# Modulation rows 4 to 9 of a hybrid diffusion step: summed on VectorE and GpSimd instead of by 32-column products on TensorE

## The chip, the cores and the metric

One core of a Trainium2 chip runs the whole step. The metric is device time in microseconds (us); the median of three runs of the kernel before is 1153.03 us. Engines: TensorE (PE, its weight loads PEld), VectorE (DVE), ScalarE (ACT), GpSimd (POOL), SyncE (SP, whose queue issues most transfers).

## The reference, cut to what matters

```python
mod = silu(c) @ w_mod + b_mod            # latent tokens; silu(c_ctx) for context tokens
shift1, scale1, gate1, shift2, scale2, gate2 = split(mod, 6)
h = rms_norm(x, g_attn) * (1 + scale1) + shift1
x = x + gate1 * token_mixing(h)          # attention, two branches, output projection
h = rms_norm(x, g_ffn) * (1 + scale2) + shift2
x = x + gate2 * expert_choice_ffn(h)     # 16 experts
y = rms_norm(x, g_final)
```

`w_mod` is 1024 x 6144 in float32. The kernel works on it in twelve "rows" of 512 columns: rows 0 to 3 are shift1 and scale1, rows 4 and 5 gate1, rows 6 and 7 shift2, rows 8 and 9 scale2, rows 10 and 11 gate2. Each row is wanted for two vectors: v = 0, the latent condition, and v = 1, the context condition. There are 512 latent and 128 context tokens, in five tiles of 128.

## The kernel before

The program of each engine is written out by hand, with semaphores between the engines; each engine executes its own list in order.

The dense part is a list of 15 matrix products, `GEMMS`, numbered j = 0 to 14. Numbers 5 to 14 follow attention: ga0, wa0, gb0, wb0 (5 to 8) make columns 0 to 511 of the merged branches, ga1, wa1, gb1, wb1 (9 to 12) columns 512 to 1023, out0 and out1 (13, 14) are the output projection. The g products have eight blocks of 128 rows of weights, the w products four. Weights arrive in chunks of 1 MB (`STREAM`, one after the other through a ring of four buffers `raw`, issued by SP as the buffer's last user finishes). A chunk is two halves `hh`; each half is passed once over the five token tiles t, with two blocks and three float32r matmuls of 512 columns for each (high times high, high times low, low times high). ScalarE makes the high part of a half (`split_hi`), VectorE the low part (`split_lo`, 1024 columns), both two halves ahead of TensorE (`half_ahead`). A product's result lies in one of six PSUM banks. For a w product VectorE frees the bank (`branch_of`: a multiply, and for gb's partner wb also an add that makes `merged`), for a g product ScalarE does (`gate_of`). So a place in the order is a triple (j, hh, t).

Rows 4 to 9 of the modulation are twelve more chunks of that stream (`MODS_AFTER`: after which chunk which of them follows). `mod_chunk` (line 787) runs each as four matmuls with the two condition vectors as stationary operand, two columns of each of four 32-column groups of the array. After a row's second chunk VectorE copies the 128 x 512 partial result out of bank 7 (`keep_row`, line 1910, counted in `s_row`).

`TURNS` says before which place TensorE does a small extra task through PSUM bank 6, one after the other: "merged" transposes one tile of the merged branches, "turn" n brings row n into columns (line 857), "spread" n, v spreads a gate1 row over all partitions (line 861). VectorE finishes each at the same place of its own list: `merged_lo` the low part of the transposed tile, `add_bias` for a turn (`turned_row`), and for a spread an add onto `gate1`, which holds the bias and is loaded by GpSimd after product 11 (lines 2325 to 2327, awaited through `s_gb`). `residual_of` multiplies the output projection by `gate1`.

`gate_step` (line 1945) sums rows 10 and 11 on VectorE already: for each block of 128 rows a scalar-times-tensor-plus-tensor instruction over 512 columns.

In the stretch between attention and the end of product 11 GpSimd has nothing to do: its list stands at the wait of line 2325. The experts follow the dense part: `expert_block` on TensorE, with weights through twenty 1 MB buffers.

Of the kernel before, what the change touches and what calls it, by code (L numbers as in the profile page):

```python
# [100 lines left out]
def halves_of(j):  # L101
# [13 lines left out]
TURNS = {(9, 1, 0): ("merged", 0), (9, 1, 2): ("merged", 1), (9, 1, 4): ("merged", 2), (9, 2, 1): ("merged", 3),  # L115
         (9, 2, 3): ("merged", 4), (10, 0, 2): ("turn", 6), (11, 0, 2): ("turn", 7), (12, 0, 2): ("turn", 8),
         (12, 0, 4): ("spread", 4, 0), (12, 1, 1): ("spread", 4, 1), (12, 1, 3): ("spread", 5, 0),
         (13, 0, 0): ("spread", 5, 1), (13, 0, 2): ("turn", 9), (13, 0, 3): ("merged", 5), (13, 0, 4): ("merged", 6),
# [4 lines left out]
GATE_STEPS = {_p: (_s // 4, _s % 4) for _s, _p in enumerate(GATE_AT)}  # L123
MOD_TURNS = [e for e in TURN_LIST if e[0] != "merged"]
# [113 lines left out]
def build(nc, x_prompt, x_sample, cache_attn_k, cache_attn_v, cache_diff_k, cache_diff_v, c, c_ctx,  # L238
# [5 lines left out]
    with ctx:  # L244
# [170 lines left out]
        s_actfn = sem("s_actfn"); s_vecfn = sem("s_vecfn"); s_vecturn = sem("s_vecturn"); s_modq = sem("s_modq"); s_tab = sem("s_tab"); s_tab2 = sem("s_tab2"); s_vec = sem("s_vec"); s_x = [sem(f"s_tokens{t}") for t in range(NT)]  # L415
# [6 lines left out]
        s_row = sem("s_row"); s_post = sem("s_post"); s_mod = sem("s_mod"); s_scale = sem("s_scale")  # L422
# [7 lines left out]
        s_kc = [sem("s_kc0"), sem("s_kc1")]; s_vc = sem("s_vc"); s_vac = sem("s_vac")  # L430
# [2024 lines left out]
```

## Time and profile before

| | us |
|---|---|
| three runs | 1152.22, 1153.03, 1153.11 |
| span of the profiled execution, first to last instruction | 1148.9 |
| what lies around the span, by the median of the runs | 4.1 |
| TensorE busy in the span | 1099.2 (96%) |
| VectorE busy | 543.8 (47%) |
| ScalarE busy | 369.2 (32%) |
| GpSimd busy | 154.4 (13%) |

The profile is one execution, taken by the hardware. The profiled execution's own device time is not listed beside its span; the runs stand 4.1 us above the span. All times below are us from the span's start, durations us unless marked ns. Matmuls overlap in the engine, so for TensorE the distance between starts tells more than a duration. In the span, attention ends near 328, products 6 to 12 run from 360.6 to 523, the experts from 625 on.

### The profile page before, as it was taken

The page shows a single profiled execution, that of the slowest core. Times are in us where ns is not written, and L with a number is a line of the kernel's source. Part 1 is how long each engine was busy: PE and PEld are TensorE (multiplying, and loading weights), DVE is VectorE, ACT ScalarE, POOL GpSimd, SP SyncE. Part 2 cuts the span into 40 slices and gives each one's busy share as a digit, 9 for nine tenths or more (in the row PEclk, how much of TensorE's full clock was granted, in tenths as well). Part 3 has the DMA queues.
Part 4 walks back from the last instruction along what each step waited for, and adds up shares of the span by engine and source line. Part 5 has one row for each costly group of instructions (what it writes and reads, how often), then busy time and mean ns, then how long its engine had stood idle before and what let it go on. Part 6 is the DMA issues. An engine that isn't in the chain of part 4 may idle for free.

```text
span 1148.9 us, 28297 instructions
## 1 busy us (share of the span) xinstructions
PE 1099.2 (96%) x12561; PEld 835.7 (73%) x12561; DVE 543.8 (47%) x993; ACT 369.2 (32%) x856; POOL 154.4 (13%) x213
## 2 busy tenths in 40 slices
PE   6999998999999999999998999999999999999983
PEld 4679887777877777777878777777777777777662
DVE  3575458889968232325877133332233222333235
ACT  4343236777754123122162321222222222211103
POOL 1342440000000000002012111111111111110020
PEclk9999999999999999999999999999999999999996
DMA  9952232212052543368989999999999999999993
GB/s 359 306 224 73 74 74 58 44 25 47 1 198 73 184 146 102 119 220 285 322 301 365 371 403 406 406 406 411 413 407 406 408 406 408 405 408 408 407 322 135
DMA packets 87467, 302.53 MB, mean 263 GB/s; under 512 B 27329, under 2 KB 28610, under 8 KB 62258
## 3 DMA queue, kind: packets, MB, share of 16 engines
q1 hardware_dynamic: 79680, 273.38, 62.0%
q0 software_dynamic: 6528, 20.10, 6.1%
q10 hardware_dynamic: 1138, 7.25, 1.7%
q8 instruction: 99, 1.62, 0.6%
q14 instruction: 22, 0.18, 0.0%
HBM read 276.86 MB, written 18.60 MB: 257 GB/s over the span
## 4 chain that ended last, share of the span: by engine, by line
PE 80%; DVE 6%; DMA 6%; issue 3%; ACT 3%; ACTq 0%; SPq 0%; POOLq 0%; POOL 0%; DVEq 0%
PE ps L1194 39%; PE ps L775 9%; PE ps L777 9%; PE ps L776 9%; PE ps L1001 3%; PE ps L985 2%; DVE neg_max L1794 2%; DMA x_dram<-y_row,rows_t 2%; PE ps L1024 1%; PE ps L1020 1%; DMA x_dram<-xn_p 1%; DVE q_lo_t L1786 1%; PE ps L797 1%; DMA raw<-in_w_in_dram 1%; DMA x_f<-x_dram 1%
## 5 line engine op out<-in xcount | busy, mean ns | idle before, releaser
L2122 DVE SCALAR_TENSOR_TENSOR y_row<-ps,gates,gate_q 32x256 f32<-32x256 f32 (+1 forms) x184 | 88.3, 480 | 237.4 <-PE ps L1194 234.9
L1549 ACT ACTIVATE h_t<-ps 128x256 f32<-128x256 f32 x48 | 15.0, 384 | 371.7 <-PE ps L1194 371.7
L775 PE MATMUL ps<-w_hi,ht 128*128 128x512 f32 (+1 forms) x320 | 124.8, 390 | 0.0
L777 PE MATMUL ps<-w_hi,ht 128*128 128x512 f32 (+1 forms) x320 | 121.8, 381 | 0.0
L776 PE MATMUL ps<-raw_lo,ht 128*128 128x512 f32 (+1 forms) x320 | 121.7, 380 | 0.0
L1194 PE MATMUL ps<-late,xe 128*32 128x256 f32 x1824 | 100.3, 379 | 0.0
L542 DVE TENSOR_TENSOR raw_lo<-raw,w_hi 128x1024 fp32r<-128x1024 f32 x48 | 57.7, 1225 | 78.5 <-ACT w_hi L537 78.0
L1194 PEld LDWEIGHTS ps<-late,xe 128*32 128x32 f32 x1824 | 71.9, 110 | 26.5
L2379 POOL DMA_INDIRECT xg<-x_dram,rows x48 | 46.1, 960 | 318.7 <-PE ps L1194 290.5
L537 ACT ACTIVATE w_hi<-raw 128x1024 fp32r<-128x1024 f32 x48 | 48.8, 1052 | 122.3 <-DMA raw<-in_w_in_dram 67.5
L1539 ACT ACTIVATE xe<-xt,mods_q 128x64 f32<-128x64 f32 x240 | 78.0, 423 | 7.6 <-DVE gates L2106 7.6
L1194 PE MATMUL ps<-raw,xe 128*32 128x256 f32 x1392 | 80.0, 379 | 0.0
L775 PEld LDWEIGHTS ps<-w_hi,ht 128*128 128x128 f32 x320 | 60.1, 188 | 16.6 <-issue 5.2
L1194 PE MATMUL ps<-raw_gate,xe 128*32 128x256 f32 x1248 | 71.3, 379 | 0.0
L1194 PEld LDWEIGHTS ps<-raw,xe 128*32 128x32 f32 x1392 | 54.9, 110 | 20.2
L777 PEld LDWEIGHTS ps<-w_hi,ht 128*128 128x128 f32 x320 | 60.0, 188 | 12.8
L1194 PE MATMUL ps<-late,ht 128*32 128x256 f32 x1200 | 67.5, 379 | 1.1 <-issue 1.1
L776 PEld LDWEIGHTS ps<-raw_lo,ht 128*128 128x128 f32 x320 | 60.2, 188 | 11.3
L1194 PEld LDWEIGHTS ps<-raw_gate,xe 128*32 128x32 f32 x1248 | 49.2, 110 | 18.2
L2113 DVE TENSOR_TENSOR h_t<-h_t,ps 128x256 f32<-128x256 f32 x48 | 19.0, 395 | 88.7 <-PE ps L1194 88.7
L1194 PEld LDWEIGHTS ps<-late,ht 128*32 128x32 f32 x1200 | 47.2, 110 | 18.9 <-issue 1.5
L1794 DVE TENSOR_REDUCE neg_max<-ps 128x1 f32<-128x768 f32 x64 | 58.2, 950 | 2.5 <-PE ps L985 2.4
(325 smaller groups left out, 1916.5 us busy)
## 6 DMA issues: line engine op xcount, KB each, us to landing
late<-in_w_exp_down_dram SPq DMA_DIRECT2D x25, 1024.0 KB, 25.6
late<-in_w_exp_up_dram SPq DMA_DIRECT2D x21, 1024.0 KB, 21.4
late<-in_w_exp_gate_dram SPq DMA_DIRECT2D x17, 1024.0 KB, 23.8
raw<-in_w_in_dram SPq DMA_DIRECT2D x16, 1024.0 KB, 5.8
raw<-in_w_exp_gate_dram SPq DMA_DIRECT2D x16, 1024.0 KB, 23.1
raw_gate<-in_w_exp_up_dram SPq DMA_DIRECT2D x14, 1024.0 KB, 26.4
raw<-in_w_exp_up_dram SPq DMA_DIRECT2D x13, 1024.0 KB, 28.0
raw_gate<-in_w_exp_down_dram SPq DMA_DIRECT2D x13, 1024.0 KB, 24.2
```

The source lines that it names most:

```text
L537: act.activation(w_hi[:, n % NHL, :], raw_half(raw, h), ACT.Copy).then_inc(s_hi, 1)
L542: dve.tensor_tensor(raw_half(raw_lo, h), raw_half(raw, h), w_hi[:, n % NHL, :].bitcast(F32), ALU.subtract)\
L775: pe.matmul(b, stat_hi(k, tt), hi[:, kk, :], start=first, stop=False)
L776: pe.matmul(b, stat_hi(k, tt), lo[:, kk, :], start=False, stop=False)
L777: mm = pe.matmul(b, stat_lo(k, tt), hi[:, kk, :], start=False, stop=last)
L985: mm = pe.matmul(bank(bb, 0, n), q[:, m % 4, t * P:(t + 1) * P], keys_t[:, x, c0:c0 + n], start=(part == 0), stop=(part == 1))
L1001: mm = pe.transpose(bank(4 + n % 3, b * P, (b + 1) * P), prob_row(2 * i + x // per)[:, kt * P:(kt + 1) * P], ident)
L1194: mm = pe.matmul(out[32 * q:32 * q + 32, :], x[:, k, :], columns_of(w, q), start=(k == 0), stop=(k == KD - 1))
L1539: a = act.activation(xe[:, n % 2, sets, k, :], xt[:, sets, k, :], ACT.Identity, scale=mods_q[:, k, v:v + 1], bias=mods_q[:, k, 2 + v:3 + v])
L1794: dve.tensor_reduce(nm, src[:, :, 0:384], AX.XY, ALU.max, negate=True).then_inc(s_max, 1)
L2122: return dve.scalar_tensor_tensor(y_row[n % 2][32 * v:32 * v + count, 256 * q:256 * q + 256], bank(b, o, o + 256, src), gates[src, n % EG, ...
L2379: pool.indirect_dma_start(xg[:, n % 2, v, :], None, x2_quarters[:, :], bass.IndirectOffsetOnAxis(ap=rows[:, v, n:n + 1], axis=0))\
```

## The change

The twelve modulation chunks leave `STREAM`. Rows 6, 7, 8, 9, 4, 5 (in that order) are summed by blocks of 128 rows of `w_mod`, eight steps a row, 48 steps in all. In each step VectorE does v = 0 with one instruction (a multiply for a row's first step, else multiply and add), GpSimd v = 1 with a multiply into `mod_tmp` and an add (for a row's first step the multiply alone). Sums of two rows at a time lie in `mod_acc`, per partition; a row's first step waits until the turn of the row two before it is done.

The weights come in 24 loads of 512 KB ("half chunks", two steps each) on GpSimd's own queue, into two buffers in turn. Load i + 2 is issued when both engines have done load i's two steps; from load 10 on the buffers lie in another place, and load 10 also waits until product 8's five merged tiles are done (`s_mrg`). The first load waits for the last head of attention to be scaled (`s_yn`). GpSimd's list for all this stands before the wait of line 2325.

VectorE's steps stand at fixed places of its list (`MOD_AT`). A turn now sums over partitions as well: for each v four matmuls with one column of ones; a spread is four matmuls with 32 columns of ones. Both wait for the row's sums on both engines (`s_sum_d`, `s_sum_p`). The places of the turns move: row 6 from (10,0,2) to (7,2,3), row 7 from (11,0,2) to (8,0,2), row 8 from (12,0,2) to (9,3,0), row 9 from (13,0,2) to (10,1,3). The spreads of rows 4 and 5 stay. Some semaphores are merged.

```diff
-MODS_AFTER = {(6, 0): [(4, 0), (4, 1)], (7, 0): [(5, 0)], (7, 1): [(5, 1)], (8, 0): [(6, 0)], (9, 0): [(6, 1)],
-              (9, 1): [(7, 0)], (10, 0): [(7, 1)], (11, 0): [(8, 0), (8, 1)], (11, 1): [(9, 0)], (12, 0): [(9, 1)],
-              }
...
-         [("gemm", j, q) for j in range(6) for q in range(chunks_of(j))]
...
+         [("gemm", j, q) for j in range(15) for q in range(chunks_of(j))]
...
-         (9, 2, 3): ("merged", 4), (10, 0, 2): ("turn", 6), (11, 0, 2): ("turn", 7), (12, 0, 2): ("turn", 8),
+TURNS = {(7, 2, 3): ("turn", 6), (8, 0, 2): ("turn", 7),
...
+         (9, 2, 3): ("merged", 4), (9, 3, 0): ("turn", 8), (10, 1, 3): ("turn", 9),
...
+MOD_ROWS = (6, 7, 8, 9, 4, 5)
+MOD_AT = [(6, 0, 1), (6, 0, 3), (6, 0, 4), (6, 1, 1), (6, 1, 3)] + \
+         [(7, _h, _t) for _h in range(4) for _t in (1, 3, 4)] + [(8, 0, 1), (8, 0, 3), (8, 0, 4), (9, 0, 3), (9, 0, 4)] + \
+         [(9, _h, _t) for _h in range(1, 4) for _t in (1, 3, 4)] + [(10, 0, 1), (10, 0, 3), (10, 0, 4), (10, 1, 1), (10, 1, 4)] + \
+         [(11, _h, _t) for _h in range(3) for _t in range(1, 5)]
+MOD_MOVED = 20
...
+        mod_acc = at("mod_acc", 143360, [P, 2, 2, NW])
+        raw_mod = [at("raw_mod0", 102400, [P, 2, 2, NW]), at("raw_mod1", 112640, [P, 2, 2, NW])]
+        mod_tmp = [at("mod_tmp0", 110592, [P, NW]), at("mod_tmp1", 120832, [P, NW])]
...
-                        for m, q in MODS_AFTER.get((j, hh // 2), []):
-                            mod_chunk(m, q)
...
-                pe.wait_ge(s_row, n + 1)
+                summed = 8 * (MOD_ROWS.index(n) + 1)
+                pe.wait_ge(s_sum_d, summed)
+                pe.wait_ge(s_sum_p, summed)
                 if event[0] == "turn":
-                    for i in range(4):
-                        mm = pe.matmul(bank(6, 2 * i, 2 * i + 2), row_of(n)[:, i * P:(i + 1) * P],
-                                       tab2[:, T_SELM - T_KEPT:T_SELM - T_KEPT + 2], start=True, stop=True)
+                    for v in range(2):
+                        for i in range(4):
+                            mm = pe.matmul(bank(6, 2 * i + v, 2 * i + v + 1), mod_sums(n, v)[:, i * P:(i + 1) * P],
+                                           ones32[:, 0:1], start=True, stop=True)
                 else:
-                    o = T_SB - T_KEPT + event[2] * P
-                    mm = pe.matmul(bank(6), tab2[:, o:o + P], row_of(n), start=True, stop=True)
+                    for q in range(4):
+                        mm = pe.matmul(bank(6, rows=slice(32 * q, 32 * q + 32)), ones32[:, :], mod_sums(n, event[2]),
+                                       start=True, stop=True)
...
+                if n == 0:
+                    dve.wait_ge(s_sum_p, MOD_MOVED)
...
+            def mod_step(step):
+
+                n, k, i = MOD_ROWS[step // 8], step % 8, step // 2
+                acc, w, c = mod_operands(step, 0)
+                dve.wait_ge(s_mod_raw[i % 2], 16 * (i // 2 + 1))
+                if k == 0:
+                    if step >= 16:
+                        dve.wait_ge(s_post, MOD_COUNT["turn", MOD_ROWS[step // 8 - 2]])
+                    dve.tensor_scalar(acc, w, c, None, ALU.mult).then_inc(s_sum_d, 1)
+                else:
+                    dve.wait_ge(s_sum_d, step)
+                    dve.scalar_tensor_tensor(acc, w, c, acc, ALU.mult, ALU.add).then_inc(s_sum_d, 1)
...
+                        if (j, hh, t) in MOD_STEPS:
+                            mod_step(MOD_STEPS[j, hh, t])
...
+            def load_mod(i):
+                n, k = MOD_ROWS[i // 4], 2 * (i % 4)
+                pool.dma_start(mod_half(i), columns(w_mod[0], NW * n, NW, k, 2)).then_inc(s_mod_raw[i % 2], 16)
+
+            def mod_step(step):
...
+                    pool.tensor_scalar(tmp[:, :], w, c, None, ALU.mult).then_inc(s_pool, 1)
+                    pool.wait_ge(s_pool, own())
+                    pool.tensor_tensor(acc, acc, tmp[:, :], ALU.add).then_inc(s_sum_p, 1)
+
+            pool.wait_ge(s_yme, 2 * HB)
+            pool.wait_ge(s_yn, HB)
+            load_mod(0)
+            load_mod(1)
+            for i in range(4 * len(MOD_ROWS)):
+                for step in (2 * i, 2 * i + 1):
+                    mod_step(step)
+                if i + 2 < 4 * len(MOD_ROWS):
+                    pool.wait_ge(s_sum_p, 2 * i + 2)
+                    pool.wait_ge(s_sum_d, 2 * i + 2)
+                    if 2 * (i + 2) == MOD_MOVED:
+                        pool.wait_ge(s_mrg, NT)
+                    load_mod(i + 2)
```

## Rows read from the trace of the kernel before

**Rows 1.** Busy time of each engine, clock, transfers; two stretches.

```profile
377.00:393.00 16.00, 16.00 (x80) 11.49 (x76) 3.44 (x4) 2.01 (x2) 0.00 (x0) 1.00 0.55 197
...
700.00:800.00 100.00, 100.00 (x1860) 73.05 (x1856) 31.56 (x75) 18.01 (x57) 14.99 (x14) 1.00 1.02 408
```

**Rows 2.** Who waited for whom: total us, times, longest.

```profile
PE ps L1194 <- DMA w_in_hi<-in_w_exp_down_dram: 3.0, 1, 3.0
...
SPq L719 <- PE ps L1194: 325.6, 150, 15.9
```

**Rows 3.** Instructions that use the ring, 360 to 523, summed: PE, PEld, DVE, ACT.

```profile
sum 163.00, PE 11.70 PEld 1.51 DVE 25.07 ACT 21.34; mean PE 1.17 PEld 0.15 DVE 2.51 ACT 2.13
```

**Rows 4.** TensorE in order of time, product 7: start, duration, what.

```profile
376.59 1.90 PE L797 MATMUL ps<-raw,vec_t 128*2 128x512 f32 x16
378.42 0.50 PE L775 MATMUL ps<-w_hi,ht 128*128 128x512 f32 x1
...
392.62 1.04 PE L797 MATMUL ps<-raw,vec_t 128*2 128x512 f32 x8
```

**Rows 5.** TensorE in order of time, the turn in product 10.

```profile
459.32 0.95 PE L857 MATMUL ps<-tab,mod_row 128*128 128x2 f32 x8
460.13 0.48 PE L775 MATMUL ps<-w_hi,yt_hi 128*128 128x512 f32 x1
```

**Rows 6.** GpSimd's elementwise instructions: ns min/median/max, first and last start.

```profile
L2254 POOL TENSOR_TENSOR kb_parts<-k_n,kb_parts x10: 733/794/1061, 151.1 to 167.2; 128x256 fp32r<-128x256 f32 x10
L2254 POOL TENSOR_TENSOR ka_parts<-k_n,ka_parts x5: 458/461/518, 116.3 to 139.7; 128x128 fp32r<-128x128 f32 x5
...
L2252 POOL CAST kb_parts<-k_n x10: 396/396/590, 150.6 to 166.7; 128x256 fp32r<-128x256 f32 x10
L2252 POOL CAST ka_parts<-k_n x5: 290/290/1207, 115.6 to 139.3; 128x128 fp32r<-128x128 f32 x5
```

**Rows 7.** GpSimd in order of time, four instructions.

```profile
119.06 1.21 POOL L2252 CAST ka_parts<-k_n 128x128 fp32r<-128x128 f32 x1
...
152.49 1.06 POOL L2254 TENSOR_TENSOR kb_parts<-k_n,kb_parts 128x256 fp32r<-128x256 f32 x1
...
164.97 0.40 POOL L2252 CAST kb_parts<-k_n 128x256 fp32r<-128x256 f32 x1 [0.69 <-PE ps L906]
165.44 0.74 POOL L2254 TENSOR_TENSOR kb_parts<-k_n,kb_parts 128x256 fp32r<-128x256 f32 x1
```

**Rows 8.** VectorE in order of time, beside the first two of rows 7.

```profile
118.89 1.23 DVE L542 TENSOR_TENSOR raw_lo<-raw,w_hi 128x1024 fp32r<-128x1024 f32 x1 [2.78 <-ACT w_hi L537]
...
152.19 0.77 DVE L473 TENSOR_TENSOR k_n<-k_n,tab 128x512 f32<-128x512 f32 x1
152.98 1.11 DVE L474 TENSOR_TENSOR k_n<-k_n,rope_d 128x512 f32<-128x512 f32 x1
```

**Rows 9.** VectorE's gate2 sums: ns min/median/max.

```profile
L1957 DVE SCALAR_TENSOR_TENSOR gate_acc<-raw_gate,vec_t,gate_acc x28: 743/746/748, 558.6 to 580.3; 128x512 f32<-128x512 f32 x28
```

**Rows 10.** VectorE in order of time: the last head scaled.

```profile
366.05 0.89 DVE L1861 SCALAR_TENSOR_TENSOR y_t<-y_t,g_dif,y_rms 128x640 f32<-128x640 f32 x1
```

**Rows 11.** GpSimd's transfers: one issue in order of time; KB, us to landing.

```profile
36.19 0.74 POOL L2272 DMA_DIRECT2D va_n<-in_cache_attn_v_dram  x1
...
lam_w<-in_lambda_q_dram POOLq DMA_DIRECT2D x2, 128.0 KB, 4.3
```

**Rows 12.** The gate1 bias: GpSimd's issue, its landing, VectorE's first add.

```profile
504.25 1.09 POOL L2327 DMA_DIRECT2D gate<-in_b_mod_dram  x2 [331.06 <-PE ps L777]
...
DMA to landing us min/median/max: 6.3/7.8/9.3
...
514.14 0.69 DVE L1943 TENSOR_TENSOR gate<-gate,ps 128x512 f32<-128x512 f32 x1 [3.05 <-DMA gate<-in_b_mod_dram]
```

**Rows 13.** Busy time and granted clock (third from the right), after or within pauses of TensorE.

```profile
616.00:618.00 2.00, 2.00 (x10) 2.00 (x11) 2.00 (x8) 0.00 (x0) 0.43 (x1) 0.50 1.04 437
...
1080.00:1084.00 4.00, 2.94 (x59) 1.85 (x52) 2.29 (x6) 0.00 (x0) 0.00 (x0) 1.00 1.01 363
```

More of the change, by code:

```diff
@@ L111 @@
 DENSE_SPLITS = len(SPLITS)
[L115 to L116 removed]
+TURNS = {(7, 2, 3): ("turn", 6), (8, 0, 2): ("turn", 7),
+         (9, 1, 0): ("merged", 0), (9, 1, 2): ("merged", 1), (9, 1, 4): ("merged", 2), (9, 2, 1): ("merged", 3),
+         (9, 2, 3): ("merged", 4), (9, 3, 0): ("turn", 8), (10, 1, 3): ("turn", 9),
          (12, 0, 4): ("spread", 4, 0), (12, 1, 1): ("spread", 4, 1), (12, 1, 3): ("spread", 5, 0),
[L118 removed]
+         (13, 0, 0): ("spread", 5, 1), (13, 0, 3): ("merged", 5), (13, 0, 4): ("merged", 6),
          (13, 1, 0): ("merged", 7), (13, 1, 1): ("merged", 8), (13, 1, 3): ("merged", 9),
@@ L412, in bank @@
             return ps[rows, 512 * b + lo:512 * b + hi]
-        s_actfn = sem("s_actfn"); s_vecfn = sem("s_vecfn"); s_vecturn = sem("s_vecturn"); s_modq = sem("s_modq"); s_tab = sem("s_tab"); s_tab2 = sem("s_tab2"); s_vec = sem("s_vec"); s_x = [sem(f"s_tokens{t}") for t in range(NT)]
+        s_actfn = sem("s_actfn"); s_vecfn = sem("s_vecfn"); s_vecturn = sem("s_vecturn"); s_tab = sem("s_tab"); s_tab2 = sem("s_tab2"); s_vec = sem("s_vec"); s_x = [sem(f"s_tokens{t}") for t in range(NT)]
         s_bc = sem("s_bc"); s_router = sem("s_router")
@@ L782, in product @@
                         after_half(hh)
-                    if hh % 2 == 1:
-                        for m, q in MODS_AFTER.get((j, hh // 2), []):
-                            mod_chunk(m, q)
-            def mod_chunk(n, q):
-                if q == 0:
-                    pe.wait_ge(s_row, n)
-                    if n == 4:
-                        pe.wait_ge(s_yme, 2 * HB)
-                chunk = CHUNK["mod", n, q]
-                pe.wait_ge(s_raw[chunk % NRAW], raw_count[chunk])
-                for g in range(4):
-                    k = 4 * q + g
-                    mm = pe.matmul(bank(7, rows=slice(32 * g, 32 * g + 2)), c_t[:, k, :],
-                                   raw[:, chunk % NRAW, g * NW:(g + 1) * NW], start=(q == 0), stop=(q == 1))
-                mm.then_inc(s_half, 2)
             def part_chunk(p, q):
@@ L1908, in residual_of @@
                    .then_inc(s_x1 if j == 14 else s_x0, 1)
-            def keep_row(n):
-                dve.wait_ge(s_half, 2 * CHUNK["mod", n, 1] + 2)
-                user = {8: ("turn", 6), 9: ("spread", 4, 1)}.get(n)
-                if user:
-                    dve.wait_ge(s_post, MOD_COUNT[user])
-                dve.tensor_copy(row_of(n), bank(7)).then_inc(s_row, 1)
             def turned_row(event):
@@ L2323, in _ @@
             pool.wait_ge(s_kout, 32)
+            def load_mod(i):
+                n, k = MOD_ROWS[i // 4], 2 * (i % 4)
+                pool.dma_start(mod_half(i), columns(w_mod[0], NW * n, NW, k, 2)).then_inc(s_mod_raw[i % 2], 16)
+            def mod_step(step):
+                n, k, i = MOD_ROWS[step // 8], step % 8, step // 2
+                acc, w, c = mod_operands(step, 1)
+                tmp = mod_tmp[0 if step < MOD_MOVED else 1]
+                pool.wait_ge(s_mod_raw[i % 2], 16 * (i // 2 + 1))
+                if k == 0:
+                    if step >= 16:
+                        pool.wait_ge(s_post, MOD_COUNT["turn", MOD_ROWS[step // 8 - 2]])
+                    pool.tensor_scalar(acc, w, c, None, ALU.mult).then_inc(s_sum_p, 1)
+                else:
+                    pool.wait_ge(s_sum_p, step)
+                    pool.tensor_scalar(tmp[:, :], w, c, None, ALU.mult).then_inc(s_pool, 1)
[14 more added lines that the diff above has]
+                    load_mod(i + 2)
             pool.wait_ge(s_half, gemm_half(11, 3) + 1)
```

61 lines of the change are left out of this document (26 added, 35 removed).

## The prediction

> **What bounds the kernel now.** I read the busy times by stretch first. In product 7's stretch TensorE is busy all 16 us, VectorE 3.4, ScalarE 2.0, GpSimd not at all; among the experts TensorE is busy all 100 us of a hundred [rows 1]. The list of waits says the same: among the experts the weights are late once, 3.0 us, and SP waits 326 us for TensorE to free buffers [rows 2]. So the loads of the experts follow TensorE, not the other way round, and their first ones are released by products 12 to 14. What TensorE gains or loses up to product 12 therefore moves all that follows, nearly one for one; nothing behind it swallows a gain or makes up a delay. The question is only when TensorE finishes product 12.
>
> **What goes.** The twelve modulation chunks occupy TensorE 11.7 us in all, laid end to end with the products [rows 3]; one chunk is about 1.0 us [rows 4]. Term: **-11.7**. VectorE's six copies out of bank 7 go too, off the path.
>
> **What the turns cost.** A turn is four weight loads with short matmuls, 0.8 us until the product goes on [rows 5]. Each load must now serve one column instead of two, so eight instead of four: 1.6. Four turns: **+3.2**. Bounds: +0 (if the second group overlaps) and +3.2; the loads were back to back before, so I take the upper. A spread by four 32-row groups I put at the old cost, as the chunk products of that same shape cost 1.0 us [rows 4]. Merged semaphores are passed at the same events as before: nothing. Transfers add up to the same 12 MB, on GpSimd's queue instead of SP's; the ring's remaining chunks come earlier, and TensorE did not wait for them: nothing.
>
> **VectorE's share** is 48 x 0.75 us [rows 9], some 36 us more in the 140 us from 367 on, where rows 1 show it a fifth busy. That is hidden as long as its steps don't hold up what stands behind them in its list: the low parts, two halves ahead, and the multiplies that free banks, half a product ahead.
>
> **GpSimd's pace** decides. No row has its instructions at 512 columns, so I extend two lines. Two inputs: 460 ns at 128 columns, 733 at 256, thus 1.28 us at 512. One input: 290 and 396 ns, thus 0.61 us for the multiply [rows 6]. For the multiply the ends are 0.61 and, if the scalar from memory counts as a second input, 1.28; one tensor is read, so I take the former. Between dependent instructions lie 0.08 us [rows 7]. A step is 0.61 + 0.08 + 1.28 + 0.08 = 2.05, a row's first step 0.69. A load's issue with two pieces a partition takes 0.74 [rows 11].
>
> The port comes on top. A GpSimd cast of 128 columns, 0.29 us elsewhere, took 1.21 when VectorE's low part had begun 0.17 before it; an add of 0.73 took 1.06 beside VectorE's 512-column add, and the next VectorE add then took 1.11, ending 0.54 after GpSimd's [rows 6 to 8]. So they take turns, instruction by instruction: a low part costs GpSimd up to 0.9, a 512-column sum up to 0.33. Per load: two sums and about three quarters of a low part, 0.66 + 0.68 = 1.3. The lower end is 0, if they never meet; but both engines work on the same load at the same time, so I take 1.3.
>
> The Trainium skill (SBUF — State Buffer, Who interferes with whom) says that a VectorE instruction with two SBUF inputs and a GpSimd instruction that reads SBUF lock each other out for the whole instruction. By that rule, the trace agrees: 0.9 and 0.33 us. Without it the sum would be the first rival's.
>
> **First wait: the turn of row 7, at (8,0,2).** GpSimd may start when the last head is scaled, 367.0 [rows 10]. A 128 KB load of its queue landed in 4.3 us, the two 512 KB loads of the bias in 6.3 and 9.3 [rows 11, 12]; for 512 KB on a quiet queue I take 5.3. First data: 372.3. Sixteen steps: 14 x 2.05 + 2 x 0.69 = 30.1; seven issues between them 5.2; port 8 x 1.3 = 10.4, of which I drop 0.5 for the times GpSimd stands waiting anyway. Row 7 is summed at **417.5**. The other loads land under the work on the one before (about 6 us a load).
>
> TensorE: product 6 ends at 376.6, product 7 took 14.2 from its start to its first chunk's end, so 1.42 a tile pass and 28.4 in all [rows 4]. Its second tile needs a bank that VectorE frees behind steps 0 to 2, now about **+1.0** late. With the turn of row 6 (1.6; its sums come at about 395, the place at about 396: no wait) and two passes it stands at (8,0,2) at 376.6 + 1.0 + 28.4 + 1.6 + 2.8 = 410.4. It waits **+7.1**.
>
> **Second wait: gate1's bias, at (12,1,1).** On from 417.5: the turn 1.6, eight passes 11.4, two VectorE instructions 1.4: product 8 is merged at 432, and load 10 may go. Steps 18 to 47 remain: 27 x 2.05 + 3 x 0.69 = 57.4, fourteen issues 10.4, port for thirty sums and ten low parts up to 19, of which I take 17, since VectorE is held up by TensorE around product 10. GpSimd is through at 517. Only then does it reach the wait for product 11 and issue gate1's bias, at 504.3 before, on that product's end [rows 12]. TensorE: products 9 to 11 take 28.4 + 14.2 + 28.4, five transposes (each no more than the 0.8 of rows 5; I take 0.65) 3.3, two turns 3.2: from 430.5 to 508; (12,0,4) 5.7 later at 513.7; (12,1,1) after the spread (1.0) and two passes at 517.5. The bias lands 6.3 to 9.9 after its issue [rows 12], I take 7.3: 524.3; VectorE's add 0.7. TensorE waits until 525, **+7.5**. (Row 5's sums are there by then.)
>
> **The clock.** Two pauses of over 7 us are new. After one pause of this trace the granted clock was 0.50, the lower of its two levels (1.2 GHz), for at least 2 us, which loses 1.0; during one of 3.0 us it stayed at 1.00 [rows 13]. Bounds 0 and about 2 each; I take **+2.5** for both.
>
> **The sum.** -11.7 + 3.2 + 1.0 + 7.1 + 7.5 + 2.5 = +9.6. The profiled span of 1148.9 would become 1158.5; the runs lie 4.1 above the span, so about **1163 us**, slower.
>
> **A page against the multiply's price.** The Trainium skill (GPSIMD Engine Reference, Elementwise — side-by-side cycle accounting) gives 769 ns for 512 elements of a good one-input loop; no run here shows it. By it the sum would be some 8 us more.
>
> **Rivals.**
> *The engines hardly collide (chance 0.17).* If VectorE's and GpSimd's instructions mostly miss each other, sixteen steps end at 372.3 + 30.1 + 5.2 = 407.6, before TensorE's 410; gate1's bias is issued as product 11 ends, as before. Only -11.7 + 3.2 remains: 1144.5, faster. It decides where GpSimd does a load in 5 us or less. For it: GpSimd's own pauses leave VectorE room. Against it: rows 7 and 8.
> *One wait only (0.13).* GpSimd loses time at row 7 but is through before product 11 ends, so the bias is in time. Then -11.7 + 3.2 + 1 + 7.1 + 1.3 = +1: 1154, no difference to be measured. It needs 5 us a load after 432.
> *Slower than I price it (0.16).* Loads that land in 6.5 us (between the two of rows 12), or a multiply near 0.8: about 7 us a load, so 6 more at row 7 and, over thirty steps, 12 more at the end; VectorE's steps then also hold up low parts. About 1180.
> *The forecast (0.54).* Two waits of 4 to 11 us: 1156 to 1173.
>
> **Chances.** Faster by over 0.2% (2.3 us, about what a measurement of this kernel can tell from no change): the first rival and a little of the second, 0.20. Within: 0.09. Slower: 0.71. The range for 8 in 10 leaves out most of the first rival and the far end of the third: 1147 to 1181; the forecast's own is 1156 to 1173.
>
> **What would show it.** In the profile after: 48 GpSimd adds near 1.3 us alone and 1.6 or more beside VectorE; TensorE waiting at a turn in product 8 for a GpSimd or VectorE sum; GpSimd's issue of gate1's bias some 9 us behind product 11's end and a wait of TensorE at the second spread; the lower clock behind each. GpSimd at 5 us a load, with no such wait, would make it wrong to the fast side; a wait for low parts in product 12 to the slow side.

## The result and the profile after

The changed kernel takes **1208.05 us** (median of four runs, 1205.98 to 1209.35) against 1152.86 for the kernel before in the same session: 1.0474 times as long, 95% interval 1.046 to 1.0489. The prediction was slower, 1163 us, with 1181 as the upper end of its range. The direction was right and the size was not: +55 us instead of +10. The profiled execution spans 1206.7 us, 57.8 more than before. (A run's device time lies about 2 us above its span, 1208.6 against 1206.7 here. So, by estimate, the profiled execution of the kernel before took near 1151, some 2 us less than the median of its runs; that is why the spans differ by 57.8 and the medians by 55.) The last merged tile is transposed at 595.34 instead of 538.89, so 56.5 of the 57.8 arise up to product 13, where the change lies.

From the list of waits of the changed kernel, TensorE in 350 to 700 (total us, times, longest), the four in its dense part that the kernel before did not have:

```profile
PE ps L850 <- POOL mod_acc L2339: 25.8, 3, 11.2
PE ps L854 <- DVE gate L1928: 9.6, 1, 9.6
PE ps L782 <- DVE raw_lo L542: 6.1, 2, 3.6
PE ps L840 <- DVE mt_lo L1872: 5.6, 2, 3.6
```

L850 is the turn: it waits for GpSimd's sums three times (7.8 at row 6, 11.2 at row 7, 6.8 at row 9), where one wait of 7.1 was forecast. L854 is the spread that waits for gate1's bias, forecast with 7.5. The other two are low parts of weights and of merged tiles, which VectorE delivers late. Together 47.1 us.

TensorE in order of time at the turn of row 6, then at that of row 8, which had no wait (start, duration, what):

```profile
402.56 3.54 PE L850 MATMUL ps<-ones,mod_acc 128*128 128x1 f32 x16 [7.81 <-POOL mod_acc L2339]
405.97 0.77 PE L782 MATMUL ps<-w_hi,ht 128*128 128x512 f32 x1
406.54 0.63 PE L783 MATMUL ps<-raw_lo,ht 128*128 128x512 f32 x1
406.96 0.63 PE L784 MATMUL ps<-w_hi,ht 128*128 128x512 f32 x1
...
411.56 0.39 PE L783 MATMUL ps<-raw_lo,ht 128*128 128x512 f32 x1
411.79 0.40 PE L784 MATMUL ps<-w_hi,ht 128*128 128x512 f32 x1
...
477.90 1.84 PE L850 MATMUL ps<-ones,mod_acc 128*128 128x1 f32 x16
479.60 0.48 PE L782 MATMUL ps<-w_hi,ht 128*128 128x512 f32 x1
```

Without a wait ahead of it a turn takes 1.70 us until the product goes on; after the wait it takes 3.41, and the products behind it start 0.43 apart instead of 0.23 until 411.2. The windows of that stretch show why (granted clock third from the right, as in [rows 13]):

```profile
394.00:402.50 8.50, 0.75 (x4) 0.27 (x2) 1.41 (x3) 0.00 (x0) 7.74 (x6) 0.72 0.32 112
402.50:406.00 3.50, 3.44 (x17) 3.47 (x17) 0.00 (x0) 0.00 (x0) 3.08 (x3) 0.50 0.42 140
406.00:411.40 5.40, 5.40 (x14) 4.24 (x15) 3.98 (x4) 0.00 (x0) 4.97 (x4) 0.50 0.26 71
411.40:415.00 3.60, 3.60 (x17) 2.92 (x16) 2.23 (x2) 1.20 (x2) 3.35 (x3) 0.99 0.12 48
```

Before it TensorE had stood still for 7.8 us; then the clock stands at its lower level (0.50, 1.2 GHz) for about 9 us. The same level shows behind four more waits, for 4 to 9 us each. In distances between starts the low clock takes 1.7 us at each of the three late turns, 0.9 at the late spread and 11.1 among the products: about 17 us. The ledger up to product 13 is then: -11.7 for the chunks [rows 3], four turns at 1.70 instead of 0.81 +3.6, waits +47.1, clock +17: **+56**, against 56.5 measured.

Why the sums are late shows in GpSimd's list, one load with its two steps (answering to [rows 7] and the issue of [rows 11]):

```profile
379.72 0.77 POOL L2323 DMA_DIRECT2D raw_mod<-in_w_mod_dram  x1 [0.30 <-POOL mod_acc L2339]
380.53 1.58 POOL L2337 TENSOR_SCALAR mod_tmp<-raw_mod,vec_t 128x512 f32<-128x512 f32 x1
382.19 1.30 POOL L2339 TENSOR_TENSOR mod_acc<-mod_acc,mod_tmp 128x512 f32<-128x512 f32 x1
383.66 1.57 POOL L2337 TENSOR_SCALAR mod_tmp<-raw_mod,vec_t 128x512 f32<-128x512 f32 x1 [0.17 <-POOL mod_acc L2339]
385.32 1.29 POOL L2339 TENSOR_TENSOR mod_acc<-mod_acc,mod_tmp 128x512 f32<-128x512 f32 x1
386.90 0.76 POOL L2323 DMA_DIRECT2D raw_mod<-in_w_mod_dram  x1 [0.30 <-POOL mod_acc L2339]
```

Here VectorE costs GpSimd nothing (it is VectorE that gives way: its sum begun at 385.42, just behind GpSimd's add, takes 1.74 us instead of 0.75), and a load still takes 7.2 us. The add has the 1.28 us that were extended from [rows 6]; the multiply takes 1.57 instead of 0.61. Over all steps (ns min/median/max):

```profile
L2337 POOL TENSOR_SCALAR mod_tmp<-raw_mod,vec_t x42: 1564/1577/3179, 374.9 to 560.3; 128x512 f32<-128x512 f32 x42
...
L2339 POOL TENSOR_TENSOR mod_acc<-mod_acc,mod_tmp x42: 1261/1292/1871, 377.8 to 562.8; 128x512 f32<-128x512 f32 x42
```

The medians lie beside the minima: more than half of GpSimd's instructions run undisturbed. From 379.72 to 432.61 seven loads are 7.6 us apart. Then GpSimd loses more, at load 10:

```profile
436.81 1.67 POOL L2339 TENSOR_TENSOR mod_acc<-mod_acc,mod_tmp 128x512 f32<-128x512 f32 x1
450.66 0.76 POOL L2323 DMA_DIRECT2D raw_mod<-in_w_mod_dram  x1 [12.18 <-DVE merged L1889]
...
563.96 1.15 POOL L2357 DMA_DIRECT2D gate<-in_b_mod_dram  x2
```

Load 10 waits for product 8's merged tiles, and product 8 is itself late, because TensorE stood at the turns for GpSimd. The last line is gate1's bias, issued at 504.25 before [rows 12] and now 60 us later.

### The profile page after: what moved, and what is told of

It is laid out like the page before. It is cut to its first block, busy times and chain, and to the rows that moved or that the text cites. A ratio compares the mean times of both kernels' runs of the same rounds, so it can differ in the third digit from the quotient of the medians.

```text
span 1206.7 us, 28467 instructions
## 1 busy us (share of the span) xinstructions
PE 1106.4 (92%) x12521; PEld 905.0 (75%) x12521; DVE 587.6 (49%) x1035; ACT 368.6 (31%) x856; POOL 320.8 (27%) x327
## 4 chain that ended last, share of the span: by engine, by line
PE 64%; POOL 13%; DMA 8%; DVE 7%; issue 4%; ACT 3%; SPq 1%; POOLq 0%; ACTq 0%; DVEq 0%
PE ps L1185 37%; POOL mod_tmp L2337 6%; PE ps L782 5%; PE ps L784 5%; PE ps L783 5%; POOL mod_acc L2339 5%; PE ps L995 2%; PE ps L979 2%; DVE neg_max L1785 2%; DMA x_dram<-y_row,rows_t 2%; PE ps L1018 1%; DMA x_dram<-xn_p 1%; POOL raw_mod L2323 1%; PE ps L1014 1%; DMA raw_first<-in_w_in_dram 1%
## 5 line engine op out<-in xcount | busy, mean ns | idle before, releaser
L1185 PEld LDWEIGHTS ps<-late,xe 128*32 128x32 f32 x1824 | 85.4, 110 | 14.9
L1185 PE MATMUL ps<-raw,xe 128*32 128x256 f32 x1392 | 88.7, 379 | 0.7 <-issue 0.6
L1185 PEld LDWEIGHTS ps<-raw,xe 128*32 128x32 f32 x1392 | 68.4, 110 | 12.7 <-issue 2.1
L1185 PE MATMUL ps<-raw_gate,xe 128*32 128x256 f32 x1248 | 77.8, 379 | 0.0
L2337 POOL TENSOR_SCALAR mod_tmp<-raw_mod,vec_t 128x512 f32<-128x512 f32 x42 | 75.5, 1797 | 5.7 <-POOL mod_acc L2339 3.1
L1941 DVE SCALAR_TENSOR_TENSOR mod_acc<-raw_mod,vec_t,mod_acc 128x512 f32<-128x512 f32 x42 | 43.2, 1029 | 68.6 <-DMA raw_mod<-in_w_mod_dram 66.7
L2323 POOL DMA_DIRECT2D raw_mod<-in_w_mod_dram x24 | 18.2, 759 | 212.9 <-DVE y_t L1852 194.5
L1185 PE MATMUL ps<-late,ht 128*32 128x256 f32 x1200 | 71.8, 379 | 1.0 <-issue 1.0
L782 PEld LDWEIGHTS ps<-w_hi,ht 128*128 128x128 f32 x320 | 60.9, 190 | 11.9 <-DVE q_n L1704 0.2
L1185 PEld LDWEIGHTS ps<-raw_gate,xe 128*32 128x32 f32 x1248 | 61.2, 110 | 9.6
L1185 PEld LDWEIGHTS ps<-late,ht 128*32 128x32 f32 x1200 | 56.3, 110 | 12.1 <-issue 1.5
```

What stands on the lines that cost most here:

```text
L782: pe.matmul(b, stat_hi(k, tt), hi[:, kk, :], start=first, stop=False)
L1185: mm = pe.matmul(out[32 * q:32 * q + 32, :], x[:, k, :], columns_of(w, q), start=(k == 0), stop=(k == KD - 1))
L1941: dve.scalar_tensor_tensor(acc, w, c, acc, ALU.mult, ALU.add).then_inc(s_sum_d, 1)
L2323: pool.dma_start(mod_half(i), columns(w_mod[0], NW * n, NW, k, 2)).then_inc(s_mod_raw[i % 2], 16)
L2337: pool.tensor_scalar(tmp[:, :], w, c, None, ALU.mult).then_inc(s_pool, 1)
```

## The experiments

The kernel before, run beside each group of experiments, stood at 1152.97 to 1153.43 us (medians).

**Four forms of the multiply.**

```diff
-                    pool.tensor_scalar(tmp[:, :], w, c, None, ALU.mult).then_inc(s_pool, 1)
+                    row = step // 8
+                    if row == 1:
+                        pool.tensor_scalar(tmp[:, :], w, 0.5, None, ALU.mult).then_inc(s_pool, 1)
+                    elif row == 2:
+                        pool.tensor_copy(tmp[:, :], w).then_inc(s_pool, 1)
+                    elif row == 3:
+                        pool.tensor_tensor(tmp[:, :], w, c.broadcast_to([P, NW]), ALU.mult).then_inc(s_pool, 1)
+                    else:
+                        pool.tensor_scalar(tmp[:, :], w, c, None, ALU.mult).then_inc(s_pool, 1)
```

> GpSimd's multiply is given four forms, one for each row: row 6 as it is (scalar per partition), row 7 by a constant of the instruction, row 8 a plain copy, row 9 tensor times tensor with the condition broadcast along the row; rows 4 and 5 as row 6. Rows 7 and 8 leave the factor out, so this run is for the durations. If the scalar read from memory is what costs, the constant and the copy take 0.6 to 0.8 us at 512 columns and row 6 keeps its 1.58. If the operation is dear whatever its scalar, the constant also takes 1.5 to 1.6 and only the copy is near 0.61. If GpSimd is simply slow at 512 columns, all forms take 1.3 to 1.6. Tensor times tensor: 1.28 in any of them.

(`row` counts in the order of the sums: 0 is row 6, 1 is row 7.) Measured: 1196.03 us in its one run. The four lines of GpSimd, ns min/median/max:

```profile
L2339 POOL TENSOR_SCALAR mod_tmp<-raw_mod x7: 1489/1492/1819, 404.6 to 426.7; 128x512 f32<-128x512 f32 x7
...
L2341 POOL COPY mod_tmp<-raw_mod x7: 608/615/1012, 432.5 to 464.3; 128x512 f32<-128x512 f32 x7
...
L2343 POOL TENSOR_TENSOR mod_tmp<-raw_mod,vec_t x7: 1041/1054/1836, 470.6 to 490.7; 128x512 f32<-128x512 f32 x7
...
L2345 POOL TENSOR_SCALAR mod_tmp<-raw_mod,vec_t x21: 1564/1577/2831, 374.3 to 548.4; 128x512 f32<-128x512 f32 x21
```

The second case: it is the operation that is dear. A constant in place of the scalar saves 0.08 us of 1.57. The copy takes 0.615, which is what the casts of [rows 6] extend to (0.61). So the extension along the columns was good, and carrying it over to another one-input operation was not. A product of two tensors, one of them a broadcast column, costs 1.05, two thirds of the operation that reads one tensor.

**GpSimd with VectorE's sums nearly gone.**

```diff
-                    dve.scalar_tensor_tensor(acc, w, c, acc, ALU.mult, ALU.add).then_inc(s_sum_d, 1)
+                    dve.scalar_tensor_tensor(acc[:, 0:8], w[:, 0:8], c, acc[:, 0:8], ALU.mult, ALU.add).then_inc(s_sum_d, 1)
```

> VectorE's sums shrink to 8 of 512 columns (the sums for v = 0 are left out), so that GpSimd has the SBUF side nearly to itself except for the low parts. Theory (GpSimd's own step of 3.1 us sets the pace, collisions add only about 0.5 us a load): a load every 7.1 us instead of 7.5, some 10 us less in all, 1198 us (1192 to 1203). Rival (the collisions of the two engines make the delay): waits fall to what was predicted or to nothing, 1145 to 1165 us.

Measured: 1198.43 us (one run), 10 less than the changed kernel, as the theory had it. A load takes 7.2 us (378.79 to 429.18, seven loads). TensorE's waits:

```profile
PE ps L850 <- POOL mod_acc L2339: 11.0, 2, 6.5
PE ps L854 <- DVE gate L1928: 9.7, 1, 9.7
PE ps L850 <- DVE mod_acc L1941: 9.7, 1, 9.7
```

In the wait put down to VectorE the two sums of row 7 end together, at 428.9; VectorE's is paced by GpSimd's loads. So the three turns still wait 20.7 us (25.8 in the changed kernel), and the wait for the bias is as before. Collisions of the two engines are real, but they are the small part.

**GpSimd without the multiply.**

```diff
-                    pool.tensor_scalar(tmp[:, :], w, c, None, ALU.mult).then_inc(s_pool, 1)
-                    pool.wait_ge(s_pool, own())
-                    pool.tensor_tensor(acc, acc, tmp[:, :], ALU.add).then_inc(s_sum_p, 1)
+                    pool.tensor_tensor(acc, acc, w, ALU.add).then_inc(s_sum_p, 1)
```

> GpSimd's multiply is left out (it adds the weights themselves, the factor of v = 1 is missing); every add, load, wait and VectorE sum stays. Theory (the multiply's 1.58 us is the excess): a load every 5 us or less, no wait at row 7's turn or one of a few us, 1148 us (1143 to 1156). Rival (collisions, or the places of the turns, or the wait for product 8 before load 10): the waits stay for the most part, 1175 us or more.

Measured: 1151.22 us (1150.05 to 1155.95), 0.9986 of the kernel before (0.9975 to 0.9997). TensorE's waits in the changed part are down to:

```profile
PE ps L850 <- DVE mod_acc L1941: 1.4, 1, 1.4
PE ps L854 <- DVE gate L1928: 1.1, 1, 1.1
```

All 24 loads, the early turns, the wait for product 8 (11.9 us of GpSimd) and VectorE's sums are still there, and the collisions too, as VectorE's line shows (median 1178 ns, 746 undisturbed in [rows 9]):

```profile
L1941 DVE SCALAR_TENSOR_TENSOR mod_acc<-raw_mod,vec_t,mod_acc x42: 741/1178/2219, 374.7 to 504.5; 128x512 f32<-128x512 f32 x42
```

With one instruction less in GpSimd's step 57 us go: neither the places nor the collisions make the delay by themselves.

**VectorE sums both conditions.**

```diff
-                pe.wait_ge(s_sum_d, summed)
-                pe.wait_ge(s_sum_p, summed)
+                pe.wait_ge(s_sum_d, 2 * summed)
...
-                    dve.wait_ge(s_sum_d, step)
-                    dve.scalar_tensor_tensor(acc, w, c, acc, ALU.mult, ALU.add).then_inc(s_sum_d, 1)
...
+                for v in range(2):
+                    acc, w, c = mod_operands(step, v)
+                    if k == 0:
+                        dve.tensor_scalar(acc, w, c, None, ALU.mult).then_inc(s_sum_d, 1)
+                    else:
+                        dve.wait_ge(s_sum_d, 2 * step - 1 + v)
+                        dve.scalar_tensor_tensor(acc, w, c, acc, ALU.mult, ALU.add).then_inc(s_sum_d, 1)
...
-                for step in (2 * i, 2 * i + 1):
-                    mod_step(step)
...
-                    pool.wait_ge(s_sum_p, 2 * i + 2)
-                    pool.wait_ge(s_sum_d, 2 * i + 2)
+                    pool.wait_ge(s_sum_d, 4 * i + 4)
```

> VectorE sums both conditions (96 instructions of 0.75 us), GpSimd only issues the loads. Theory (GpSimd's arithmetic is the bound and VectorE has the room): no TensorE wait at the turns, and the prediction's plain terms remain, -11.7 for the chunks and +3.6 for the turns: 1145 us (1142 to 1150), faster than the kernel before. Rival (the early turns, the two buffers and the wait for product 8 are the bound, whoever sums): waits of TensorE at the turns in products 7 and 8 of 5 us and more stay, 1160 us or more.

Measured: **1145.36 us** (1143.97 to 1146.25), 0.9929 of the kernel before (0.9912 to 0.9945). This version beats both. The 8.0 us gained are the two plain terms, 11.7 for the chunks less 3.6 for the turns, to 0.1 us. VectorE's sums and TensorE's waits in it:

```profile
L1941 DVE SCALAR_TENSOR_TENSOR mod_acc<-raw_mod,vec_t,mod_acc x84: 741/748/765, 374.2 to 495.0; 128x512 f32<-128x512 f32 x84
```

```profile
PE ps L840 <- DVE mt_lo L1871: 0.8, 1, 0.8
PE ps L853 <- DVE gate L1927: 0.6, 1, 0.6
```

With GpSimd out of the way none of the 84 exceeds 765 ns. In the changed kernel the same line shows what GpSimd's instructions do to VectorE:

```profile
L1941 DVE SCALAR_TENSOR_TENSOR mod_acc<-raw_mod,vec_t,mod_acc x42: 741/848/1794, 373.3 to 556.9; 128x512 f32<-128x512 f32 x42
```

**The multiply as tensor times tensor.**

```diff
-                    pool.tensor_scalar(tmp[:, :], w, c, None, ALU.mult).then_inc(s_pool, 1)
+                    pool.tensor_tensor(tmp[:, :], w, c.broadcast_to([P, NW]), ALU.mult).then_inc(s_pool, 1)
```

> GpSimd's multiply written as tensor times tensor, with the condition broadcast along the row; all else as in the changed kernel. Theory (the time follows GpSimd's pace per load): the multiply takes 1.05 us instead of 1.57, a load 6.9 us instead of 7.5, and the total falls to about 1189 us (1183 to 1195). Rival (what counts is the collision of two-tensor instructions with VectorE, of which there are now twice as many): no gain or a loss, 1205 us or more.

Measured: 1186.42 us (1185.14 to 1187.17), a load every 6.6 us (379.52 to 425.90, seven loads). The time follows the pace: by the means over all 42 steps the multiply fell from 1.80 to 1.17 us and the add rose from 1.43 to 1.55; 42 times the difference is 21, and the total falls by 21.6.

**The multiply at the price that the prediction took.**

```diff
-                    pool.tensor_scalar(acc, w, c, None, ALU.mult).then_inc(s_sum_p, 1)
+                    pool.tensor_copy(acc, w).then_inc(s_sum_p, 1)
...
-                    pool.tensor_scalar(tmp[:, :], w, c, None, ALU.mult).then_inc(s_pool, 1)
+                    pool.tensor_copy(tmp[:, :], w).then_inc(s_pool, 1)
```

> GpSimd's multiply replaced by a copy (0.615 us, which is the price that the prediction took for the multiply; the factor of v = 1 is left out, in the first steps of the rows too). It tests the rest of the prediction's sum. If the multiply's price is the one step that failed: a load every 6 to 6.3 us, a wait of some 7 us at row 7's turn, a second one for the bias, 1163 us (1158 to 1168). If the other terms failed as well (waits at more places, the clock): 1172 us or more. If the port's price was too high: 1155 us or less.

Measured: 1170.28 us (1169.63 to 1172.12), between the first two cases. TensorE's waits:

```profile
PE ps L854 <- DVE gate L1928: 9.8, 1, 9.8
PE ps L850 <- POOL mod_acc L2339: 7.8, 1, 7.8
...
PE ps L782 <- DVE raw_lo L542: 1.2, 1, 1.2
PE ps L782 <- DVE merged L1885: 1.0, 1, 1.0
```

This is the profile that the prediction described: one wait at row 7's turn (7.1 forecast), the wait for the bias (7.5 forecast), 1.0 us for a bank in product 7. Seven loads from 377.81 to 419.72 are 6.0 us apart, which was the forecast. From load 10's issue (438.56) to the last sum (524.3) GpSimd needs 85.7 us; the prediction had 432 to 517, that is 85. The copy and the add exceed their undisturbed 0.615 and 1.28 us by 0.29 and 0.22 on average, so the collisions cost 1.0 us a load, against 1.3 in the prediction; an undisturbed load takes 5.1 us (438.56 to 443.68), against 4.84 by the prediction's terms. What is left of the 7 us is in sizes: the waits 19.8 instead of 15.6, the clock behind two of them 5.6 instead of 2.5, the turns 3.6 instead of 3.2.

**gate1's bias by SP's queue.**

```diff
                     sp.wait_ge(s_half, gemm_half(11, 3) + 1)
+                    for v in range(2):
+                        sp.dma_start(gate1[:, v, :], b_mod[:, 2 * D:3 * D].to_broadcast([P, D])).then_inc(s_graw[0], 16)
                     for q in range(4):
                         gate_chunk(q)
...
-                dve.wait_ge(s_gb, 32)
+                dve.wait_ge(s_graw[0], 48)
...
-            pool.wait_ge(s_half, gemm_half(11, 3) + 1)
-            for v in range(2):
-                pool.dma_start(gate1[:, v, :], b_mod[:, 2 * D:3 * D].to_broadcast([P, D])).then_inc(s_gb, 16)
```

> gate1's bias is loaded from SP's queue as product 11 ends, not by GpSimd behind its 48 steps; all else as in the changed kernel. Theory (the bias's place behind GpSimd's work costs the last wait of 9.6 us and the low clock behind it): TensorE passes the second spread at once and waits under 2 us for row 5's sums at the third: 1197 us (1194 to 1200). Rival (another thing is as late as the bias, the sums of row 5 or VectorE's adds): 1204 us or more.

Measured: 1197.33 us (1194.14 to 1199.56). The wait at the spread falls from 9.6 to 0.2 us, and 10.7 us go:

```profile
PE ps L784 <- DVE raw_lo L542: 8.8, 1, 8.8
PE ps L856 <- DVE gate L1930: 0.2, 1, 0.2
```

So the bias's place behind GpSimd's steps is a loss of its own, about a fifth of the whole.

**The turns later.**

```diff
-TURNS = {(7, 2, 3): ("turn", 6), (8, 0, 2): ("turn", 7),
+TURNS = {(8, 0, 2): ("turn", 6),
...
-         (9, 2, 3): ("merged", 4), (9, 3, 0): ("turn", 8), (10, 1, 3): ("turn", 9),
-         (12, 0, 4): ("spread", 4, 0), (12, 1, 1): ("spread", 4, 1), (12, 1, 3): ("spread", 5, 0),
-         (13, 0, 0): ("spread", 5, 1), (13, 0, 3): ("merged", 5), (13, 0, 4): ("merged", 6),
+         (9, 2, 3): ("merged", 4), (10, 1, 1): ("turn", 8), (11, 3, 2): ("turn", 9),
+         (12, 1, 4): ("spread", 4, 0), (13, 0, 0): ("spread", 4, 1), (13, 0, 1): ("spread", 5, 0),
+         (13, 0, 2): ("spread", 5, 1), (13, 0, 3): ("merged", 5), (13, 0, 4): ("merged", 6),
```

(Row 7's turn goes to (9,2,0) in the same way.)

> The turns go to later places, near the time at which GpSimd has the sums (row 6 at (8,0,2), row 7 at (9,2,0), row 8 at (10,1,1), row 9 at (11,3,2), the spreads at (12,1,4) and (13,0,0) to (13,0,2)), with gate1's bias on SP's queue as in the run before. VectorE's steps keep their places. Theory (GpSimd's pace of 7.5 us a load sets the end wherever the turns stand): the waits leave the turns, GpSimd's pause of 12.2 us for product 8 goes, but VectorE's steps of products 9 to 11 wait for loads, its low parts come late, and TensorE waits for these: 1188 us (1182 to 1195). Rival (the early places of the turns make the delay): 1155 us or less.

Measured: 1196.11 us (1194.54 to 1196.87), only 1.2 less than with the bias alone moved, and a little above the expected range. No wait stands at a turn now; TensorE waits elsewhere:

```profile
PE ps L784 <- DVE raw_lo L542: 16.9, 2, 12.1
PE ps L784 <- issue: 6.6, 1, 6.6
PE ps L784 <- DVE sig L1889: 4.9, 1, 4.9
PE ps L842 <- DVE mt_lo L1874: 4.2, 2, 3.7
```

VectorE's list holds its steps at fixed places, so with late loads it is VectorE's other work, low parts above all, that comes late. The 6.6 us named "issue" lie ahead of product 8. The profile names no releaser for them, but the times do: two sums of VectorE waited 5.8 us for a load, the low part behind them in its list ended at 411.39, and TensorE went on at 411.49. VectorE in order of time:

```profile
407.45 2.81 DVE L1943 SCALAR_TENSOR_TENSOR mod_acc<-raw_mod,vec_t,mod_acc 128x512 f32<-128x512 f32 x2 [5.76 <-DMA raw_mod<-in_w_mod_dram]
410.18 1.21 DVE L542 TENSOR_TENSOR raw_lo<-raw,w_hi 128x1024 fp32r<-128x1024 f32 x1
```

TensorE's next product:

```profile
411.49 0.77 PE L784 MATMUL ps<-w_hi,yt_hi 128*128 128x512 f32 x1 [6.62 <-issue]
```

GpSimd still waited 9.8 us for product 8, where the expectation had that gone.

**TensorE kept busy in its pauses**, three times, since the first two missed.

```diff
+                for _ in range({("turn", 6): 65, ("turn", 7): 130, ("turn", 9): 55, ("spread", 4, 1): 90}.get(event, 0)):
+                    pe.matmul(bank(7, 0, P), ident, ident, start=True, stop=True)
                 pe.wait_ge(s_sum_d, summed)
```

> Ahead of the waits at the turns of rows 6, 7 and 9 and at the second spread TensorE runs 65, 130, 55 and 90 small products (128x128, 0.105 us each in the stretch after routing) into an unused bank, so that it does not stand still and its clock should stay up; nothing else is changed. The clock losses behind the four pauses add up to about 16 us by their rows. If each is a loss of its own: 1192 us. If GpSimd's chain sets the time and TensorE only waits for it again a little longer, what is won behind the turns of rows 6 and 9 is waited away, and only that behind row 7 (3.1 us, because product 8's end releases GpSimd's load 10) and behind the last spread (2.5 us) counts: 1202 us (1200 to 1205).

Measured: 1246.39 us (1245.01 to 1247.13). A product took 0.226 us and not 0.105, because the trace holds two records for each; so they ran on after the sums were there. The run says nothing about the clock.

> The run with small products ahead of the waits once more, with half their number (32, 64, 28 and 48): the first run showed 0.226 us for each of them, not 0.105 (the trace keeps two records for one product), so that they were longer than the waits. Expected as before: 1192 us if each pause's clock loss (16 us in sum) is a loss of its own; 1202 us (1200 to 1205) if GpSimd's chain sets the time and only the losses behind row 7's turn and the last spread count.

Measured: 1213.93 us (1213.54 to 1217.03). TensorE in order of time at the second spread:

```profile
565.78 12.46 PE L846 MATMUL ps<-tab 128*128 128x128 f32 x96 [7.30 <-DVE gate L1930]
```

The small products stand behind the pause here, not in it: the turn first waits for bank 6, which VectorE frees when the bias has come. A miss of the edit again, worth 12.4 us.

```diff
+                for _ in range({("turn", 6): 34, ("turn", 7): 60, ("turn", 9): 28, ("spread", 4, 1): 36}.get(event, 0)):
+                    pe.matmul(bank(7, 0, P), ident, ident, start=True, stop=True)
                 before = TURN_LIST.index(event) - 1
                 if before < 0:
```

> The small products stand ahead of every wait of the turn now (in the second run those of the spread stood behind a wait for bank 6, so that TensorE waited 7.3 us and then ran 12.4 us of them); 34, 60, 28 and 36 of them. If each pause's clock loss is a loss of its own: 1192 us. If GpSimd's chain sets the time: 1202 us (1199 to 1205), which is also the second run's 1213.9 less the 12.4.

Measured: 1203.81 us (1201.2 to 1206.03), 4.2 less than the changed kernel. By the rows about 6 of the 17 us of low clock stayed: behind a wait for a low part (10.7 us), behind one for a merged tile (3.5 us), neither of which the edit fills, and behind row 7's turn, where TensorE had run small products for 14 us and then stood still for 1.6 us:

```profile
435.00:441.00 6.00, 6.00 (x18) 4.94 (x18) 4.36 (x5) 0.00 (x0) 5.33 (x3) 0.50 0.30 87
```

So some 11 us of low clock went and 4 of the time. It fits the second case: TensorE back at full clock only reaches the next wait sooner. From the first load's issue to the last sum GpSimd took 194.9 us, against 196.6 in the changed kernel; the rest of the gain lies behind the last spread, where the clock stayed at 1.00 this time. The loss behind row 7's turn, which the second case counts among the gains, was not won back, so the run bears on that case less sharply than it was meant to.

**VectorE for both, and the bias by SP's queue.** The edits of those two runs together.

> VectorE sums both conditions and gate1's bias comes by SP's queue. In the run with VectorE alone TensorE still waited 0.6 us for the bias and 0.8 us for a merged tile. If these are the last losses of the change: 1144.5 us (1143 to 1146), at most 1 us better than that run. If something else is left that waits for GpSimd's queue: below 1142 us.

Measured: 1147.24 us (1145.28 to 1148.25), 0.9949 of the kernel before (0.9936 to 0.9963): no better than VectorE alone, whose interval it overlaps. TensorE waits longer for the bias there than with GpSimd's queue:

```profile
PE ps L855 <- DVE gate L1929: 2.1, 1, 2.1
```

In this edit VectorE awaits the bias together with the first 1 MB chunk of gate2 on SP's queue (the count of 48 in the edit of the bias alone); the chunks land in 12.5 us at the median, the bias alone in 6.5. With GpSimd's queue free of late work the move has nothing to gain.

## Why the prediction was right in direction and wrong in size

- **Chunks, -11.7, and turns, +3.2.** Right: the run without GpSimd's arithmetic gains 8.0 us; a turn measured 1.70 against 1.6 forecast.
- **VectorE's share hidden.** Right where loads come in time. In the changed kernel its steps waited 92 us for loads, and low parts behind them cost TensorE 11.7 us; the sum had no term for that, though the rival "slower than I price it" and the signs of being wrong named it.
- **GpSimd's pace: the step that failed.** "For the multiply the ends are 0.61 and, if the scalar from memory counts as a second input, 1.28; one tensor is read, so I take the former." It measured 1.57, above both ends. Neither the scalar nor the second input explains it: with a constant it is 1.49, and a real second tensor, broadcast, takes 1.05. From load 10 on the steps left are 27 with an add and three without; 27 x 0.96 + 3 x 0.96 is 29 us, and GpSimd took 113.3 (450.66 to 564.0) instead of 85. Row 7 was summed at 432.3 instead of 417.5; 16 multiplies times 0.96 are 15. That it comes out so well is in part luck: up to there collisions cost about 7 us instead of 9.9, and the gaps that the prediction left out (0.17 us instead of 0.08 behind an add, 0.30 ahead of an issue) about 3.
- **A second fault of that step:** its upper end, 1.28, was named and then left out of the range. Over those thirty steps alone it would have given 20 us more, and the range stopped at 1181. The only GpSimd rows of that operation before the change were 128x1 to 128x8, far too narrow to price it, which was a reason to keep the high end.
- **Port, 1.3 us a load.** Near, for the pace that it was priced for: 1.0 in the run with the copy. In the changed kernel the means exceed the undisturbed 1.57 and 1.28 by 0.23 and 0.15 us, 0.7 a load, and the run without VectorE's sums gave back 10 us.
- **First wait, +7.1.** With the multiply at 0.61 it is 7.8, so the working was sound; in the changed kernel row 6 was late as well, and the two turns cost 19.0. The loop behind it, TensorE held at the turns, product 8 late, load 10 late, the prediction had (load 10 at 432). It came at 450.7; GpSimd's pause there, 12.2 us, is hardly longer than without the multiply (11.9).
- **Second wait, +7.5.** Right in place and cause: 9.6, and moving the bias takes it away. The landing, put at 7.3 us, was 4.5 here and 7.1 in the run with the copy.
- **The clock, +2.5.** Mis-sized even with two pauses (5.6 in the run with the copy); with five it is 17 by rows. Much of that is not time of its own, because GpSimd was the bound: where 11 of the 17 us went, 4 came out of the total. Behind the lower bound of 0 stands a misreading: the row of [rows 13] for 1080 to 1084 holds no pause of 3.0 us but one of 1.1 (2.94 of 4.00 us are busy). The pause of 3.0 us in the kernel before ended at 1120.8, and the lower clock followed it as well:

```profile
1120.84 3.36 PE L1194 MATMUL ps<-w_in_hi,ht 128*32 128x256 f32 x32 [3.03 <-DMA w_in_hi<-in_w_exp_down_dram]
```

The granted clock behind it (0.57 over four us, third from the right):

```profile
1121.00:1125.00 4.00, 4.00 (x48) 2.08 (x44) 2.33 (x4) 3.93 (x7) 0.00 (x0) 0.57 0.50 199
```

- **The rival "slower than I price it"** (0.16, about 1180, "a multiply near 0.8") had the mechanism with half the price; the rival in which the engines hardly collide was nearer on the collisions and wrong on the result.

The Trainium skill (GPSIMD Engine Reference, Elementwise — side-by-side cycle accounting) gives 769 ns for 512 elements as the best case, a tight loop without branches. The copy is faster (615 ns) and the multiply by a scalar twice as slow (1577 ns); the measurement decides, and that figure would have moved the sum by 8 us, not by 45.

Open is why the scalar form is dear on GpSimd.

## What to carry to other kernels

Price an instruction on GpSimd from a row of the same operation at the same width; where there is none, keep the dearest neighbour in the range and allow for more, since here one form of a multiply cost 1.57 us and another 1.05, and the dearest neighbour stood at 1.28. When an engine is added as a partner, multiply its step by the number of steps and compare that with the time until the result is wanted (here 24 loads of 7.6 us, 182 us, against some 140): if it does not fit, moving the consumer helps little (here 1.2 us). An idle share in the profile does not say which idle engine is the better one; VectorE, which already worked in this stretch, did the same step in a quarter of the time (0.75 us against 3.1) and needed no partner.

## What the runs showed of the hardware

- GpSimd, 128x512 float32, undisturbed: copy 0.615 us, tensor times broadcast column 1.05, tensor plus tensor 1.28, tensor times constant 1.49, tensor times scalar per partition 1.57. VectorE's multiply and add over the same tensor in one instruction: 0.75.
- Two 512 KB transfers on GpSimd's queue landed in 4.5 us in the changed kernel, issued when the DMA engines stood nearly idle (share 0.01 in 560 to 564), and in 7.1 in the run with the copy (share 1.04 in 522 to 524). On SP's queue they landed in 6.5 to 7.8.
- GpSimd and VectorE slow each other when both are at work: VectorE's 512-column sum, 0.75 us alone, has a median of 0.85 in the changed kernel and of 1.18 where GpSimd does adds only.
- After a pause of 7.8 us TensorE ran about 9 us at the lower clock (0.50), through a turn that itself kept it busy; after a pause of 2.0 us, behind a late merged tile, products followed at their usual 0.23 us. The length of a pause alone does not tell: of two of 3.6 us in the changed kernel, one left the clock at 1.00 (474.6 to 478), the other was followed by 0.50 (545.5 to 551), and in the third run with small products one of 1.6 us, at row 7's turn, was followed by 0.50.
